# Differential attention with concurrent row halves and split key turns; delta rates through four column quarters

## The reference, cut to what matters

```python
def diff_attention(q, k, v, lam):
    s = jnp.einsum('bqhtd,bmhtd->bhtqm', q, k) * DIFF_DIM ** -0.5   # t: two halves of 64 features
    p = jax.nn.softmax(s, axis=-1)
    a = p[:, :, 0] - lam * p[:, :, 1]
    return jnp.einsum('bhqm,bmhe->bqhe', a, v)
...
beta = jax.nn.sigmoid(to_dir(p_beta))           # p_beta, p_alpha: hx @ w_in, 16 columns each
g = -jnp.exp(a_log) * jax.nn.softplus(to_dir(p_alpha) + dt_bias)
```

## Time and profile before

| | us |
| --- | --- |
| median of 3 runs | 2713.06 (2712.33 to 2715.16) |
| the profiled execution | 2720.91 |
| its span | 2719.1 |
| span of `first_block` | 0 to 238.7 |
| span of `diff_attention` | 238.7 to 363.2 |

### The profile page before, as it was taken

How to read it: one execution, slowest core, us unless ns; L and a number is a source line. 1 busy time by engine, 2 the same in 40 slices (tenths; PEclk the granted TensorE clock), 3 DMA queues, 4 the chain that set the end, 5 groups by cost and what they waited for, 6 DMA issues and landing times. The chain is left out here.

```text
span 2719.1 us, 37721 instructions
## 1 busy us (share of the span) xinstructions
PE 2434.4 (90%) x16456; PEld 1660.6 (61%) x16456; DVE 908.9 (33%) x1769; ACT 544.8 (20%) x1284; POOL 222.8 (8%) x269
## 2 busy tenths in 40 slices
PE   4999989969975999999999999897676599999998
PEld 2656655548874855555569998455422385444698
DVE  2124712267751422222220022326655623222111
ACT  2102631242202311111110021114411022111110
POOL 1000000027740000000000000000011200000000
PEclk8898989989997999999999999998887799999999
DMA  8251001000012101011025556110100011121354
GB/s 299 95 184 31 1 23 40 0 1 4 4 31 96 62 31 62 31 62 62 31 60 162 168 177 212 62 62 16 59 0 0 0 62 62 62 93 62 87 149 138
DMA packets 190786, 193.46 MB, mean 71 GB/s; under 512 B 4970, under 2 KB 174622, under 8 KB 190430
## 3 DMA queue, kind: packets, MB, share of 16 engines
q1 hardware_dynamic: 177950, 145.55, 17.6%
q0 software_dynamic: 11584, 42.24, 4.3%
q10 hardware_dynamic: 1088, 3.26, 0.3%
HBM read 188.94 MB, written 2.10 MB: 70 GB/s over the span
## 5 line engine op out<-in xcount | busy, mean ns | idle before, releaser
L1402 PE MATMUL banks<-mem 128*128 128x512 f32 x1312 | 618.1, 591 | 0.0
L1736 PE MATMUL banks<-mem 128*128 128x128 f32 x3520 | 405.4, 277 | 11.2 <-PEq L1325 9.9
L1736 PEld LDWEIGHTS banks<-mem 128*128 128x128 f32 x3520 | 400.7, 194 | 21.2 <-issue 19.8
L461 DVE SCALAR_TENSOR_TENSOR mem<-banks,mem 128x511 f32<-128x511 f32 (+1 forms) x168 | 106.0, 660 | 750.3 <-ACT mem L1473 327.0
L1402 PEld LDWEIGHTS banks<-mem 128*128 128x128 f32 x1312 | 247.8, 189 | 171.9 <-issue 153.2
L1405 PEld LDWEIGHTS banks<-mem 128*128 128x128 f32 x672 | 127.1, 189 | 162.0 <-issue 162.0
L1405 PE MATMUL banks<-mem 128*128 128x256 f32 x672 | 200.1, 378 | 0.0
L1821 PE MATMUL banks<-mem 128*128 128x512 f32 x400 | 192.9, 614 | 5.3 <-issue 5.3
L1471 ACT ACTIVATE mem<-banks,mem 128x512 f32<-128x512 f32 x88 | 60.7, 690 | 629.9 <-PE banks L1405 373.5
L1347 PE MATMUL banks<-mem 128*128 128x256 f32 x640 | 144.8, 387 | 13.2 <-PEq L671 11.1
L873 PE MATMUL banks<-mem 64*64 64x64 f32 x3840 | 127.4, 220 | 18.5 <-DVE mem L1149 11.4
(11 more groups left out here) (307 smaller groups left out, 2743.3 us busy)
## 6 DMA issues: line engine op xcount, KB each, us to landing
mem<-in_ffn_w_up SPq DMA_DIRECT2D x44, 1024.0 KB, 5.4
mem<-in_ffn_w_down SPq DMA_DIRECT2D x64, 704.0 KB, 6.6
mem<-in_w_mod POOLq DMA_DIRECT2D x40, 1024.0 KB, 7.4
mem<-in_ab_w_in SPq DMA_DIRECT2D x14, 1024.0 KB, 5.5
mem<-in_w_mod SPq DMA_DIRECT2D x8, 1024.0 KB, 14.8
mem<-in_cd_w_in SPq DMA_DIRECT2D x8, 1024.0 KB, 5.7
mem<-in_ab_w_out SPq DMA_DIRECT2D x4, 1024.0 KB, 9.2
mem<-in_cd_w_out SPq DMA_DIRECT2D x4, 1024.0 KB, 5.1
```

The lines of the kernel that those rows point to most:

```text
L461: step = v.scalar_tensor_tensor(out[:, 1:n], src[:, 0:n - 1], tap(0), out[:, 1:n], ALU.mult, ALU.add)
L1402: last = nc.tensor.matmul(c.ps[:, bank, :], w[:, k, :], ht[:, k, 0:N_X], start=k == 0, stop=k == KT - 1)
L1736: last = c.nc.tensor.matmul(c.ps[:, n % self.n_banks, 0:128], hidden[:, k, t * 128:(t + 1) * 128], w, start=k == 0, stop=k == FT - 1)
```

## The change

In `diff_attention`:

- Both halves' scores are issued together, interleaved, into 1536 neighbouring PSUM columns (3 banks); two units have such a buffer each. One bank is shared by the halves: half 0's last part waits until half 1's first part is complete (`bank_shared`).
- PE's order in iteration i is scores(i + 1), values(i - 2), transposes(i - 1). The four image tiles are transposed first, the two context tiles after `kept` of the unit before, since the single values buffer shares their bank. ACT copies them in two parts.
- DVE no longer scales the second probabilities (L626). It adds them with the factor -lam-ratio in one step, and ACT divides by the row sum when it copies the values' product.
- The squares are taken on GpSimd, summed on DVE in two instructions (one in iteration 19, one at the end), and the norm is Sqrt on ACT and a reciprocal on DVE.

In `first_block` the rates' weights become the stationary operand, 32 columns at a time, with the 8 contraction steps spread over four column quarters of PE's output; ACT copies the four partial sums to SBUF (`keep`), and 48 small matmuls (`pick`) add the quarters and put chunks and heads in place. Each later step hangs one tile later.

```diff
+                cut = 1024 - N_ALL
+                parts = [(1, N_X, N_ALL), (0, N_X, N_ALL)] if first else \
+                    [(0, 0, N_X), (1, 0, cut), (1, cut, N_ALL), (0, N_X, N_ALL)]
+                for s, a, b in parts:
+                    r = slice(64 * s, 64 * s + 64)
+                    if (s, a, first) == (0, N_X, 0):
+                        pe.wait_ge(bank_shared, u + 1)
+                    last = nc.tensor.matmul(score(u, s)[:, a:b], qk[r, h, q * 128:(q + 1) * 128], qk[r, 4 + h, a:b],
+                                            start=True, stop=True)
+                    if b == N_ALL:
+                        last.then_inc(scored[s], 1)
+                    elif s:
+                        last.then_inc(bank_shared, 1)
...
+            scores(0)
+            for i in range(n_units + 2):
+                if i + 1 < n_units:
+                    scores(i + 1)
+                if 0 <= i - 2:
+                    values(i - 2)
+                if 0 <= i - 1 < n_units:
+                    turn_unit(i - 1)
...
+            def keep(u):
+                act.wait_ge(valued, u + 1)
+                nc.scalar.activation(by_unit[:, place(u), :], valued_at, ACT.Copy,
+                                     scale=inverse[:, u % 4, 0:1]).then_inc(kept, 1)
+            for i in range(n_units + 2):
+                if i >= 2:
+                    turned_copy(i - 2)
                 if i < n_units:
                     exps(i, 0)
                     exps(i, 1)
+                if i >= 2:
+                    keep(i - 2)
+            act.wait_ge(summed, 2)
+            nc.scalar.activation(rstd, rstd, ACT.Sqrt, bias=EPS, scale=1.0 / 128).then_inc(rooted, 1)
...
+            for i in range(-1, n_units + 1):
+                if 0 <= i - 1:
+                    weigh(i - 1)
+                if i + 1 < n_units:
+                    for s in range(2):
+                        maxima(i + 1, s)
+                if i == n_long + 3:
+                    sum_squares(slice(0, TX), n_long)
+            sum_squares(slice(TX, TT), n_units)
...
-        for t in range(TT):
+        for bank, tokens in zip(banks, (slice(0, N_X), slice(N_X, N_ALL))):
+            n = tokens.stop - tokens.start
             for k in range(KT):
-                last = c.nc.tensor.matmul(c.ps[:, bank, 32 * t:32 * t + 32], ht[:, k, 128 * t:128 * t + 128],
-                                          self.weights[:, k, :], start=k == 0, stop=k == KT - 1)
+                p = slice(32 * (k % 4), 32 * (k % 4) + 32)
+                last = c.nc.tensor.matmul(c.ps[p, bank, 0:n], self.weights[:, k, :], ht[:, k, tokens],
+                                          start=k < 4, stop=k >= 4)
...
+    def pick(self, pe, bank):
+        pe.wait_ge(self.kept, 1)
+        for s in range(STEPS):
+            for r in range(2):
+                t0 = chunk_of(s, r)
+                for hh in range(2):
+                    last = c.nc.tensor.matmul(c.ps[64 * hh:64 * hh + 64, bank, (2 * s + r) * 8:(2 * s + r) * 8 + 8],
+                                              self.groups[:, t0:t0 + CHUNK], pick[:, r, hh, :], start=True, stop=True)
```

More of the change, by code:

```diff
@@ L101, in constant_tables @@
                     pick[what * 16 + direction * 8 + 2 * p + hh, direction, hh, what, p] = 1
-    put("pick", pick, 32)
+    put("pick", np.tile(pick.reshape(32, 32), (4, 1)))
     row_of = np.zeros((4, 32, 2, 128))
@@ L513, in _, with scores @@
         def _(pe):
-            def scores(u, s):
+            def scores(u):
                 q, h, first = units[u]
[L516 to L523, removed]
+                if u >= 2:
+                    pe.wait_ge(exped, 2 * (u - 2) + 2)
+                cut = 1024 - N_ALL
[11 more added lines that the diff above has]
+                        last.then_inc(bank_shared, 1)
@@ L525, in turn_unit, with turn_tile @@
+            def turn_tile(u, m):
+                return nc.tensor.transpose(turn[:, m * 128:(m + 1) * 128], prob[:, u % 3, 0, m * 128:(m + 1) * 128],
+                                           c.tab["ident"])
             def turn_unit(u):
                 pe.wait_ge(weighed, u + 1)
+                if not units[u][2]:
+                    if u:
+                        pe.wait_ge(turned_sb, u)
+                    for m in range(TX):
+                        last = turn_tile(u, m)
+                    last.then_inc(turned_x, 1)
@@ L527, in turn_unit @@
                 if u:
[L528 to L531, removed]
+                    pe.wait_ge(kept, u)
+                for m in range(TX, TT):
+                    last = turn_tile(u, m)
                 last.then_inc(turned_ps, 1)
@@ L601, in _ @@
                                      scale=c.stat[:, 204:205]).then_inc(written, 1)
+        @block.gpsimd
+        def _(pool):
+            for u in range(n_units):
+                pool.wait_ge(kept, u + 1)
+                nc.gpsimd.tensor_tensor(squares[:, place(u), :], by_unit[:, place(u), :], by_unit[:, place(u), :],
+                                        ALU.mult).then_inc(squared, 1)
         @block.vector
@@ L614, in maxima, with weigh @@
                                         ALU.mult).then_inc(maxed, 1)
[L616 to L632, removed]
+            def weigh(u):
+                first = units[u][2]
+                b = u % 4
+                dve.wait_ge(exped, 2 * u + 2)
+                if u >= 4:
+                    dve.wait_ge(kept, u - 3)
+                link(nc.vector.reciprocal(inverse[:, b, :], total[:, b, :]))
+                link(nc.vector.scalar_tensor_tensor(ratio[:, b:b + 1], inverse[:, b, 1:2], c.stat[:, 203:204],
+                                                    total[:, b, 0:1], ALU.mult, ALU.mult))
+                nc.vector.scalar_tensor_tensor(prob[:, u % 3, 0, first:N_ALL], prob[:, u % 3, 1, first:N_ALL],
+                                               ratio[:, b:b + 1], prob[:, u % 3, 0, first:N_ALL],
+                                               ALU.mult, ALU.add).then_inc(weighed, 1)
@@ L2158, in spread @@
         eng.wait_ge(self.came, self.LOADED)
[L2159 to L2169, removed]
+        eng.wait_ge(self.picked, 1)
+        self.dve(eng, v.tensor_copy(self.raw.rearrange("p s v -> p (s v)"), c.ps[:, bank, 0:192]))
         for hh in range(2):
```

118 lines of the change are left out of this document (60 added, 58 removed).

## The result

The changed kernel takes 2687.89 us (median of four runs: 2678.73, 2688.38, 2688.09, 2687.69), against 2714.11 us for the kernel before beside it (2712.33 to 2718.59). The ratio is 0.9893, with a 95% interval of 0.9873 to 0.9914: 26.2 us faster (23 to 34 by the interval). The forecast was 34.4 us and 2679.

The account below looks back on a forecast made before the run. TensorE, busy 90% of the span, was taken to bound the kernel. Terms 11.2 + 17.9 + 3.5 + 0.3 + 1.5 = 34.4 us off 2713.1 gave 2678.7, rounded 2679; range 2669 to 2697.

Parts of the forecast that it names:

- The likeliest case: Whole kernel: 34.4 us faster, 2679 us, own range 2671 to 2685; chance 0.54.
- Rates: First block: old product and slow clock behind it removed, 17.2 us, less new product 2.7 and pick 3.3; net 11.2 us.
- pick is dear: Rival, first block: pick takes 0.100 us per instruction and the clock falls, 9.5 us lost, 2688; chance 0.1.
- Long units: Attention's steady part: period about 3.85 us in place of 5.32, over 12.2 periods 17.9 us saved (bounds 2.7 and 19.8).
- the wait on the shared bank is over after about 0.6 us: Long units' scores: half 0 needs the bank at 0.86 us, so the wait costs nothing; slot 1.57 us.
- Start: Attention's first three units: clock lost as before, but less work per unit at half rate; 3.5 us less (bounds 0 and 5).
- Short units: Attention's 8 short units: period 2.25 for 2.5 us saves 2.0, against the sum of squares; net 0.3 (bounds -3 and +3).
- Tail: Attention's end: square on GpSimd, Sqrt table load ahead of its wait; gain 1.5 us (bounds 0.2 and 2).
- the marks: Trace signs: product and pick about 3 us each, scores 1.6, period 3.8 to 4.0, stage about 101, ScalarE wait below 0.3.
- three bounds named as refuting: Long units: period above 4.5 us, scores 1.9 us or more, or clock below 1.00 in the steady part.
- starts in program order: Rival: a pass waits until all earlier-issued passes have started; 5.2 us lost in attention, 2.6 in rates; 2687, chance 0.1.
- the wait holds TensorE's queue: Rival, long units: shared-bank wait holds the whole queue or halves do not overlap; period 5.1 us, 2694, chance 0.1.

Follow-up runs that it names:

- sum_late: Changed kernel with the sum over the image units' squares moved from iteration 19 to after the last unit's work; 2683.83 us, ratio to before 0.9887.
- attn_only: Kernel before with the new differential attention alone, its rates left as they were; 2695.59 us, ratio to before 0.9928.
- serial_halves: Changed kernel with the score halves one after the other: all of half 0, a wait, then half 1; 2713.51 us (one run).
- swap_order: Changed kernel with half 1's first part (256 columns) issued before half 0's 512 columns; 2682.24 us, ratio to before 0.9879.
- own_banks: Changed kernel with no bank shared by the halves, no wait between them, and one score buffer for all units; 2748.51 us (one run).
- short_bank: Changed kernel with half 1's first part issued first, the long sum last, and short units' values product in the transposes' unused bank; 2671.89 us, ratio 0.9848.

## Why the prediction was off in size

The likeliest case had the sign and the mechanism right. The whole range, 2669 to 2697, holds 2687.89; the likeliest case's own, 2671 to 2685, doesn't. Its sum was 34.4; the two stages gave 28.2. Term by term:

- *Rates*: 11.2 forecast, 11.3 in the stretch. Product 2.61 for 2.7, pick 2.91 for 3.3, clock 1.00 behind both. The rival "pick is dear" is out. That the sum fits so closely is luck: 1.0 us came from the clock in the first tile, and 1.3 went to the longer wait for L304's weights, against "transfers keep their places relative to the tiles". Six of the other seven kernels with the new rates, whose first tile has 4.9 to 5.7 us at 0.50, take 164.6 to 165.2 us, a gain of 10.0 to 10.5; the seventh, `sum_late`, has 3.4 us there and 163.9. A small misreading beside it: the slow clock outlived the old product by 4.6 us and not 4.3, worth 0.1.
- *Long units*: 17.9 forecast, 12.2 x (5.32 - 4.25) = 13.1 measured. The step that failed is "the wait on the shared bank is over after about 0.6 us, and half 0 needs it at 0.86, so it is free". It is over at 1.20 and costs 0.33 in every unit, 4.0 in 12.2. The bare slot was overrated by 0.08, the saved change of mode was 0.1 and not 0.2, and the wait for `kept` takes 0.19 for 0.15.
- *Start*: 3.5 forecast, 4.7 measured up to unit 2's transposes, with the clock low for 3.4 us. It is a matter of luck as well: `attn_only` has 6.3 here, with no loss of clock.
- *Short units*: 0.3 forecast, -2.8 measured. The period was right (2.24 for 2.25), the gap too (1.47 for "1 to 2 us"). What failed is the netting of the sum's 2.2 us against its cover: the clock behind it was left to the bounds (-3), and it did fall. `serial_halves` shows that it need not have.
- *Tail*: 1.5 and 1.5, with the table load hidden as read from the earlier trace rows.

The attention's four terms add to 16.5; the other 0.4 of the 16.9 lies where the long units pass into the short ones.

Of the marks, the scores (1.6 us), the period (3.8 to 4.0) and the stage's length (101 us) failed, with 1.82, 4.25 and 107.6; the wait for ScalarE (below 0.3 us) holds in the long units, 0.26, and not in the short ones, 0.55. None of the three bounds named as refuting was passed. With the order swapped the stage is 101.4 and the period 3.93, as was forecast, but the length fits by luck: a start that keeps its clock makes up for short units that lose it.

The rival "starts in program order" named 2687, next to what was measured, and is wrong all the same. Its slots, worked out for the two orders, are 1.71 and 1.50 us, so `swap_order` alone doesn't exclude it; `own_banks` does, with 1.49 in the order for which it has 1.71, and so do the starts in the traces. The Trainium skill (TensorE: Matmul & The Clock Gate, The mechanism) has matmuls strictly in order both in start and in end. On starts the trace disagrees here too (half 1's first pass 0.01 us after half 0's, its second 0.21 us before half 0's second, which was issued earlier); on the order in which ends are signalled, `swap_order` and `own_banks` agree with it. The prediction set the rule aside as a whole, where only its first half was refuted.

The rival "the wait holds TensorE's queue" was the right place with the wrong mechanism and price: the halves do overlap, half 1's 512 columns stream while half 0's last part waits, and it is 0.33 a unit and not 1.25.

## What to carry to other kernels

Matmuls on different row groups run beside each other, but count on their semaphore signals in the order of issue: issue first what somebody waits for, and the short one ahead of the long. On an engine that feeds TensorE in short periods, a single long instruction costs its gap (1.1 us here) and can cost the clock of what follows (it did in three kernels of four, some 4 us in the changed one); put it where TensorE waits anyway. When work is taken out of TensorE's stream, look at the transfers behind it: 1.3 us of the rates' gain went to a wait for weights. And a change of 1% is read from the stretches that it touches: here the rest of the program moved by 10.8 us between two profiles with the same instructions.

## What the runs showed of the hardware

- A completion signal waits for matmuls issued earlier that run on other rows: the same wait is over at 1.20 us with a 512-column matmul issued ahead of its own, and costs nothing with its own issued first.
- 96 short matmuls without a gap (0.100 us each) lost the clock in the kernel before; the 96 of the pick at 0.030 each, in 2.9 us, did not, in any of the eight kernels that have it. `attn_only`, with the old 96, lost the clock in them again.
- In the short units a gap of 1.47 us is followed by 23.9 us at 0.50, though TensorE waits 0.55 in each period before it at 1.00; in `serial_halves` a gap of 1.48 us at the same place is followed by 8.4 us at 1.00. At the attention's start the same code with the same wait of 2.57 us loses the clock for 3.4 us in the changed kernel and not at all in `attn_only`. In the attention of `short_bank`, with TensorE busy for 11.49 of 14 us, the clock stays at 1.00 to 309.6.
